# A modulation product on one Trainium2 core: from accumulated rows and TensorE sums to VectorE products with a running sum

## What is computed

```python
mod = jax.nn.silu(c) @ w_ada[i] + b_ada[i]
mod_c = jax.nn.silu(c_ctx) @ w_ada[i] + b_ada[i]
sh1, sc1, g1, sh2, sc2, g2 = jnp.split(mod[:, None, :], N_MOD, axis=-1)
csh1, csc1, cg1, csh2, csc2, cg2 = jnp.split(mod_c, N_MOD, axis=-1)
...
hc = modulate(rmsnorm(xc, norm1_g[i]), csh1, csc1)
k_c, v_c = jnp.split(hc @ w_in[i][:, NA_WIDTH:3 * NA_WIDTH], 2, axis=-1)
...
h = modulate(rmsnorm(x, norm1_g[i]), sh1, sc1)
...
x = x + g1 * gated_merge(gna, ghy, y_na, y_hy, w_na_o[i], w_hy_o[i], w_out[i])
h2 = modulate(rmsnorm(x, norm2_g[i]), sh2, sc2)
x = x + g2 * swiglu(h2, ffn_w1[i], ffn_w3[i], ffn_w2[i])
```

## Time and profile before

| | us |
|---|---|
| three runs | 1608.90, 1612.44, 1613.04; median 1612.44 |
| the profiled execution, its own time | 1610.57 |
| its span in the profile | 1608.8 |
| mean granted clock of TensorE | 0.99 |
| VectorE busy | 1002.3 |
| ScalarE busy | 692.4 |
| HBM read and written over the span | 179.67 MB and 21.00 MB, 125 GB/s |

### The profile page before, as it was taken

One profiled execution on the slowest core, in us unless ns is written; L12 is line 12 of the kernel. 1 busy time (PEld: TensorE's weight loads), 2 busy tenths in 40 slices (PEclk: granted clock), 3 DMA queues, 4 the chain that ended last, 5 costly groups with the idle time before them and its releaser, 6 DMA issues. The chain is left out here.

```text
span 1608.8 us, 21150 instructions
## 1 busy us (share of the span) xinstructions
PE 1558.5 (97%) x8536; PEld 1316.6 (82%) x8536; DVE 1002.3 (62%) x1453; ACT 692.4 (43%) x1020; POOL 428.8 (27%) x371
## 2 busy tenths in 40 slices
PE   6999998999999999999999999999999999999997
PEld 5768886788888887888988778887788999999886
DVE  7675457778887476334775643338855688885324
ACT  5644346736433333323533344443445544443322
POOL 0024325523421010100060022214442655550002
PEclk9999999999999899999999999999999999999999
DMA  7342112452444254231446433215462122224221
GB/s 301 105 144 92 70 69 79 158 214 74 157 163 151 105 209 156 106 105 57 152 157 247 123 103 108 105 40 184 136 220 90 54 104 105 106 106 157 82 76 53
DMA packets 46684, 202.05 MB, mean 126 GB/s; under 512 B 14480, under 2 KB 14736, under 8 KB 27962
## 3 DMA queue, kind: packets, MB, share of 16 engines
q1 hardware_dynamic: 37346, 172.04, 29.6%
q0 software_dynamic: 8704, 28.30, 4.9%
q10 hardware_dynamic: 536, 0.35, 0.1%
HBM read 179.67 MB, written 21.00 MB: 125 GB/s over the span
## 5 line engine op out<-in xcount | busy, mean ns | idle before, releaser
L572 PE MATMUL ps<-xh,whi 128*128 128x512 f32 (+1 forms) x1136 | 404.8, 356 | 11.3 <-DVE xl L1898 8.4
L574 PE MATMUL ps<-xh,wlo 128*128 128x512 f32 (+1 forms) x1136 | 397.7, 350 | 0.0
L573 PE MATMUL ps<-xl,whi 128*128 128x512 f32 (+1 forms) x1136 | 397.6, 350 | 0.0
L1854 DVE TENSOR_TENSOR wlo<-raw,whi 128x2048 fp32r<-128x2048 f32 x89 | 217.5, 2444 | 142.5 <-ACT whi L1218 142.4
L1218 ACT ACTIVATE whi<-raw 128x512 fp32r<-128x512 f32 (+1 forms) x191 | 233.0, 1223 | 156.8 <-PE ps L574 86.8
L572 PEld LDWEIGHTS ps<-xh,whi 128*128 128x128 f32 x1136 | 215.9, 190 | 51.3 <-issue 22.2
L574 PEld LDWEIGHTS ps<-xh,wlo 128*128 128x128 f32 x1136 | 216.4, 190 | 30.5
L573 PEld LDWEIGHTS ps<-xl,whi 128*128 128x128 f32 x1136 | 216.0, 190 | 28.2
L2733 POOL TENSOR_TENSOR act<-xr 128x512 f32<-128x512 f32 x22 | 40.0, 1818 | 199.7 <-DVE xr L2296 199.0
L2296 DVE SCALAR_TENSOR_TENSOR xr<-ps,pc,xr 128x511 f32<-128x511 f32 x88 | 65.2, 746 | 41.5 <-ACT xr L1218 39.9
L2629 DVE TENSOR_TENSOR wlo<-raw,whi 128x512 fp32r<-128x512 f32 x98 | 77.4, 820 | 0.7 <-ACT whi L1218 0.7
(11 more groups left out here) (477 smaller groups left out, 3497.0 us busy)
## 6 DMA issues: line engine op xcount, KB each, us to landing
raw<-in_w_in SPq DMA_DIRECT2D x35, 1024.0 KB, 5.2
raw<-in_ffn_w SPq DMA_DIRECT2D x33, 1024.0 KB, 4.8
raw<-in_ada SPq DMA_DIRECT2D x24, 1024.0 KB, 4.8
raw<-in_w_up SPq DMA_DIRECT2D x22, 1024.0 KB, 4.8
raw<-in_w_down SPq DMA_DIRECT2D x11, 1024.0 KB, 4.8
xd<-X POOLq DMA_DIRECT2D x8, 512.0 KB, 6.6
td<-vr POOLq DMA_DIRECT2D x16, 256.0 KB, 3.6
raw<-td SPq DMA_DIRECT2D x4, 1024.0 KB, 4.8
```

Source lines behind the costliest of these rows:

```text
L572: pe.e.matmul(o, lh, rh, start=start, stop=False)
L573: pe.e.matmul(o, lh, rl, start=False, stop=False)
L574: return pe.e.matmul(o, ll, rh, start=False, stop=stop)
L1854: up(ve.e.tensor_tensor(lo, raw[conv_at[j] % 3][:, :], hi.bitcast(F32), ALU.subtract), "wlo")
```

## The change

The modulation weight is stored transposed: a chunk now holds two blocks of 128 outputs (on the partitions) by 1,024 inputs. silu(c_ctx) and silu(c) are written once to a small HBM buffer `csd` (ScalarE, 2,048 single numbers), and read back as rows repeated on all partitions: `cb` (2,048 wide, in the buffer of `ch`) before the up stage, `cb2` (silu(c) alone, in the buffer of `xh`) after up tile 43. `ada(n)` is now two blocks with one `tensor_tensor_reduce` each (two in group 0: context and token), which multiplies chunk and row and leaves the sum over the inputs as a column of `mod` or `small`. The product itself goes back over the chunk (or into `spent`) and isn't used.

TensorE's sums are gone; `Fills.skip` moves the rotation on by as many banks as they took. The chunks of group 0 sit at up steps 4, 5, 7, 8, 10, 11, 13, 14, and the other 16 in the down stage (`ADA_DOWN`), behind the split of piece k + 4. The context's `channels(8)` and `(9)` move from after step 13 to after step 17. The gates are columns now, and ScalarE stores them to `gated` with two transfers of 1,024 single numbers, before the query copies. GpSimd's three kinds of gate transfers go, and its two row loads into `bc` come before the up stage.

```diff
@@ the plan
-ADA_UP = (1, 2, 3, 5, 6, 7, 9, 10, *range(12, 20))
-ADA_IN2 = (1, 2, 3, 4, 5, 5, 6, 6)
+ADA_UP = (4, 5, 7, 8, 10, 11, 13, 14)
+ADA_DOWN = (*range(4), *range(5, 10), *range(11, 18))
...
-    several("w_down", 11)
...
+    for i in range(11):
+        plan.append(("w", ins["w_down"][i]))
+        for n, k in enumerate(ADA_DOWN):
+            if k // 2 == i - 1:
+                plan.append(("ada", ins["ada"][8 + n]))
+    several("w_in2", 20)
@@ tensor_program: the sums, and where they were called
-            def ada(g):
-
-                b = take(("adc", g), "mod", (2, 5, 6)[g])
-                pe.wait_ge(sig["cst"], 1)
-                pe.wait_ge(sig["ada"], ada_no(8 * g + 7))
-                for o, src, n_ in ((0, acc_c, 16), (16, acc_x, 16)) if g == 0 else ((0, bc, 8),):
-                    c0 = 1024 if g == 1 else 0
-                    for i in range(n_):
-                        m = pe.e.matmul(b[:, o + i:o + i + 1], src[:, c0 + P * i:c0 + P * i + P], onesf[:, 0:1],
-                                        start=True, stop=True)
-                done(m, ("adc", g))
-                for h in range(2) if g else ():
-                    b = take(("adr", g, h), "adrow", 2 * (g - 1) + h + 1)
-                    c0 = 512 * h + (1024 if g == 2 else 0)
-                    done(pe.e.matmul(b[0:1, :], onesf[:, 0:1], bc[:, c0:c0 + 512], start=True, stop=True), ("adr", g, h))
...
-                        ada((11, 20).index(2 * j2 + part))
-                if j2 == 6:
+                        fills.skip(1 if j2 < 10 else 3)
+                if j2 == 8:
@@ scalar_program
+            ac.wait_ge(sig["cs"], 1)
+            ac.e.dma_start(bass.AP(csd.tensor, 0, [[1, P], [P, 16]]), cs[:, :], allow_slow_non_contiguous=True).then_inc(sig["brow"], 16)
...
+            ac.wait_ge(sig["brow"], 16)
+            ac.e.dma_start(cb, bass.AP(csd.tensor, 0, [[0, P], [1, 2 * D]])).then_inc(sig["brow"], 16)
...
-                    if inst == 0 and k == 3:
-                        ac.wait_ge(sig["gated"], 16)
...
+            tile(("up", 43))
+            ac.e.dma_start(cb2, bass.AP(csd.tensor, 0, [[0, P], [1, D]])).then_inc(sig["brow"], 16)
...
+            ac.wait_ge(sig["adrow"], 2)
+            for i in range(2):
+                ac.e.dma_start(bass.AP(gated.tensor, D * i, [[1, P], [P, 8]]),
+                               small[:, 257 + 8 * i:265 + 8 * i], allow_slow_non_contiguous=True).then_inc(sig["gated"], 16)
@@ vector_program, ada(n)
-                for dst, c in ((acc_c, 0), (acc_x, 8)) if g == 0 else ((bc, 0),):
-                    col = cs[:, c + k:c + k + 1]
-                    if k == 0:
-                        m = ve.e.tensor_scalar(dst[:, :], raw[i % 3][:, :], col, None, ALU.mult)
...
-                        m = ve.e.scalar_tensor_tensor(out=dst[:, :], in0=raw[i % 3][:, :], scalar=col, in1=dst[:, :],
-                                                      op0=ALU.mult, op1=ALU.add)
+                ve.wait_ge(sig["brow"], 32 if n < 8 else 48)
+                for b in range(2):
+                    w = r[:, D * b:D * b + D]
+                    if n < 8:
+                        ve.wait_ge(sig["ada"], ada_no(n - 1) - 3 + 2 * b if n else 0)
+                        for o, dst, c in ((0, spent[b], cb[:, 0:D]), (16, w, cb[:, D:2 * D])):
+                            col = o + 2 * n + b
+                            up(ve.e.tensor_tensor_reduce(dst, w, c, 1.0, 0.0, ALU.mult, ALU.add, mod[:, col:col + 1]), "ada")
                     else:
+                        up(ve.e.tensor_tensor_reduce(w, w, cb2, 1.0, 0.0, ALU.mult, ALU.add, ada_col(2 * n + b)), "ada")
@@ vector_program, pieces
                     if k + 4 < NFF:
                         one(k + 4)
+                    if inst == 0 and k in ADA_DOWN:
+                        ada(8 + ADA_DOWN.index(k))
@@ the weight as stored
-    g["ada"] = a["w_ada_2"][0].reshape(8, P, 3, 2048).transpose(2, 0, 1, 3).reshape(24, P, 2048)
+    g["ada"] = a["w_ada_2"][0].T.reshape(24, 2, P, D).transpose(0, 2, 1, 3).reshape(24, P, 2048)
```

More of the change, by code:

```diff
@@ L71, in group, with skip @@
         return 1
+    def skip(self, n, pool="all"):
+        self.turn[pool] += n
     def take(self, pe, key, sem, value, pool="all"):
@@ L125, in ada_no @@
 def ada_no(a):
-    return 2 * a + 2 if a < 8 else a + 9
-ADA_UP = (1, 2, 3, 5, 6, 7, 9, 10, *range(12, 20))
-ADA_IN2 = (1, 2, 3, 4, 5, 5, 6, 6)
+    return 4 * (a + 1) if a < 8 else 2 * (a + 1) + 16
+ADA_UP = (4, 5, 7, 8, 10, 11, 13, 14)
+ADA_DOWN = (*range(4), *range(5, 10), *range(11, 18))
 KC0 = (0, 8, 24, 32)
@@ L339, in build, with ada_col @@
         ncd = dram("ncd", [8, S])
+        def ada_col(i):
+            g, k = divmod(i, 8)
+            x, at_ = (mod, 8 * g + 8 + k) if g in (3, 4) else (small, 257 + k + (8 if g == 5 else 0))
+            return x[:, at_:at_ + 1]
         def pcol(name, i=0, rows=P):
@@ L1975, in ada @@
             def ada(n):
[L1977 removed]
                 i = ada_at[n]
+                r = raw[i % 3]
                 ve.wait_ge(raw_sem[i % 3], 16 * (i // 3 + 1))
[L1980 to L1986, removed]
[L1987 to L1995 removed]
+                ve.wait_ge(sig["brow"], 32 if n < 8 else 48)
[6 more added lines that the diff above has]
+                            up(ve.e.tensor_tensor_reduce(dst, w, c, 1.0, 0.0, ALU.mult, ALU.add, mod[:, col:col + 1]), "ada")
+                    else:
+                        up(ve.e.tensor_tensor_reduce(w, w, cb2, 1.0, 0.0, ALU.mult, ALU.add, ada_col(2 * n + b)), "ada")
             def ada_sums(g):
[L1998 removed]
                 ba, n1, n2 = PCOLS["b_ada"], PCOLS["norm1_g"], PCOLS["norm2_g"]
                 if g == 0:
+                    ve.wait_ge(sig["ada"], ada_no(7))
                     for o in (0, 16):
[L2002 removed]
+                        up(ve.e.tensor_tensor(mod[:, o:o + 16], mod[:, o:o + 16], pc[:, ba:ba + 16], ALU.add), "mod")
                     ve.wait_ge(sig["mod"], 2)
@@ L2007, in ada_sums @@
                     return
-                if g == 1:
-                    up(ve.e.tensor_tensor(mod[:, 32:40], b[:, 0:8], pc[:, ba + 24:ba + 32], ALU.add), "mod")
-                else:
-                    up(ve.e.tensor_tensor(mod[:, 40:48], b[:, 0:8], pc[:, ba + 32:ba + 40], ALU.add), "mod")
-                    ve.wait_ge(sig["mod"], 6)
-                    up(ve.e.scalar_tensor_tensor(out=mod[:, 40:48], in0=mod[:, 40:48], scalar=1.0, in1=pc[:, n2:n2 + 8],
-                                                 op0=ALU.add, op1=ALU.mult), "mod")
-                ve.wait_ge(sig["brow"], 16 * g)
-                r = row2 if g == 1 else row3
-                for h in range(2):
-                    b = tile(("adr", g, h))
-                    c = slice(512 * h, 512 * h + 512)
-                    up(ve.e.tensor_tensor(r[0:1, c], b[0:1, :], r[0:1, c], ALU.add), "adrow")
+                ve.wait_ge(sig["ada"], ada_no(23))
+                up(ve.e.tensor_tensor(mod[:, 32:40], mod[:, 32:40], pc[:, ba + 24:ba + 32], ALU.add), "mod")
+                up(ve.e.tensor_tensor(mod[:, 40:48], mod[:, 40:48], pc[:, ba + 32:ba + 40], ALU.add), "mod")
+                ve.wait_ge(sig["mod"], 6)
+                up(ve.e.scalar_tensor_tensor(out=mod[:, 40:48], in0=mod[:, 40:48], scalar=1.0, in1=pc[:, n2:n2 + 8],
+                                             op0=ALU.add, op1=ALU.mult), "mod")
+                for i, a in enumerate((16, 40)):
+                    x = small[:, 257 + 8 * i:265 + 8 * i]
+                    up(ve.e.tensor_tensor(x, x, pc[:, ba + a:ba + a + 8], ALU.add), "adrow")
             def gate_input(g, rows, bias):
@@ L2859, in gpsimd_program @@
                 affine(t)
+            po.wait_ge(sig["xb"], 4)
+            po.e.dma_start(bcg[:, :], rows_of(ins["rows"], 4)).then_inc(sig["rows"], 16)
+            po.e.dma_start(bcb[:, :], rows_of(ins["rows"], 5)).then_inc(sig["rows"], 16)
             for j2 in range(11):
```

57 lines of the change are left out of this document (10 added, 47 removed).

## The result

The changed kernel takes **1593.26 us** (median of 4 runs, 1591.28 to 1597.04), the kernel before 1611.78 us (4 runs, 1608.90 to 1613.04): a ratio of **0.9894, with a 95% interval from 0.988 to 0.9908**. The forecast was 1591.5 us, 0.9870 of the median it started from. Between the two medians lie 18.5 us, where a gain of 20.9 was predicted. The profiled execution took 1591.28 us, with a span of 1589.5: 19.3 us less than the span before.

A forecast was written before the change was run, and what follows sets the result against it. TensorE, busy 97% of the span, was taken as the bound. Gains of 13.5 + 3.7 + 3.7 = 20.9 us, with added work hidden, took 1612.4 to 1591.5 us; range 1586.5 to 1602.

The forecast's parts named there:

- Terms 1 to 3: At the three places where TensorE sums the modulation: removing the sums gains 13.5 + 3.7 + 3.7 = 20.9 us.
- Term 1: First group's sums at 516 us: 10.65 us of products plus 2.85 at the 1.2 GHz level, 13.5 us gained.
- The price of a product with running sum: On VectorE: 1,024 columns and the read of the sum take 0.69 + 0.53 + 0.08 = 1.30 us a piece.
- some 5 us more: VectorE's added work over all chunks, claimed hidden because VectorE isn't the bound.
- The rival of the slow product: VectorE's product is slow from SBUF: at 2.0 us a piece the whole gain is used up; chance 0.08.
- The cover in the up stage: Up stage: VectorE's chunk work stays hidden between low-half splits, with 1.4 us left at the tightest place; cost 0.
- The cover in the down stage: Down stage with 16 added chunks: VectorE does 8.9 us per 11.24 us period, splits and loads in time; cost 0.
- The rival of starving: Down stage: loads take 8 us instead of 4.8, 10 us lost, giving 1601.5 us; chance 0.10.
- The small transfers at 0: ScalarE's single-number transfers near 52 and 797 us: cost between 0 and 7 us, taken as 0.
- Whose waits are for work long done: Rotation of TensorE's eight banks: skipped places cost no instruction and keep the rotation, whose waits are already met.
- The move of the chunks: Group 0's chunks at other up steps, the other 16 in the down stage: nothing booked for moving them.
- The gain isn't kept: At the context's keys or attention TensorE arrives earlier but waits for the same end of another chain: 1612 us; chance 0.04.

The follow-up runs named there:

- experiment 1: Kernel before with TensorE's sums cut to one one-column product per accumulator and per row half, VectorE's multiply-adds kept: 1593.61 us, ratio 0.9897.
- experiment 2: Kernel before with only the first group's sums cut to one product per accumulator: 1601.02 us, ratio 0.9942.
- experiment 8: Changed kernel with group 0's chunks back at up steps 1, 2, 3, 5, 6, 7, 9, 10: 1600.10 us, ratio 0.9924.
- Experiment 6: Changed kernel with two more VectorE products per block in the up stage, doubling the work per chunk: 1625.70 us, ratio 1.0091.
- experiment 7: Changed kernel with one more VectorE product per block in the down stage: 1602.88 us, ratio 0.9946.
- experiment 5: Changed kernel without the skipped bank places, so every later bank is another one: 1599.84 us, ratio 0.9934.
- 9: Changed kernel with group 0's chunks at up steps 2, 3, 5, 6, 7, 9, 10, 11: 1590.74 us, ratio 0.9894.

## Why the prediction was right, step by step

- *Terms 1 to 3.* Right in sum: the pair at 947 us shows 20.6 us, once the lead of 0.24 from ahead of the places is taken off, where the sum less the wait is 20.5; experiment 1 gets the same time without anything else of the change. Term 1 alone: 13.5 of 13.5 in the changed kernel, 13.1 of 13.3 in experiment 2. That a clock at the 1.2 GHz level belonged to the sums' price is shown by experiment 2, in which it stays at 1.00. By the medians the gain is 18.5 us, 2.4 less than predicted; that the forecast is only 1.8 us from the measured time owes 0.7 us to luck, the median of three runs that it started from having been that much above the median of four.
- *The price of a product with running sum.* Right in kind, 13% too high: 1.30 us was 0.69 + 0.53 + 0.08, and from start to start it is 1.15. The product takes 1.22 us, the read lies beside the next one. A chunk of group 0 takes 4.58 us, not 5.2. The "some 5 us more" for VectorE isn't what the prediction's own prices add up to (8 x 0.5 + 16 x 0.2 is 7.2 us); the page shows 1.5. The rival of the slow product (from 2.0 us a piece) fell, but not by as much as the median says: beside GpSimd it takes 3.4 us (experiment 8), and one at 476.75 us of the changed kernel, beside GpSimd's multiplication into `act`, took 2.31.
- *The cover in the up stage.* Right: no wait from 404 to 620 us. Experiment 6 makes the same chain late by doubling the work, though not in four equal parts.
- *The cover in the down stage.* Right in direction, with a wait of 0.4 us; its slack was worked out too small (experiment 7: 9.6 us for an expected 15). The rival of starving fell: the loads of `w_down` land in 5.2 us (median), not 8.
- *The small transfers at 0.* Right: their issues take 0.41 us and 1.01 us for two, inside idle time that didn't grow. The Trainium skill ("DMA: Bandwidth & Descriptors", Rules for kernel authors) speaks against a strided last dimension; the extra packets are there, 4,432 of them where the single numbers are 4,096, but on no path. Queue q10 of the page (packets, MB, share of the DMA engines) had 536 packets before and has now:

```profile
q10 hardware_dynamic: 4968, 1.94, 0.5%
```

- *"Whose waits are for work long done".* This was said of the bank rotation, and holds only because the change keeps it. It was an explanation too weak for what the skipped places do: without them one wait is 7.24 us (experiment 5).
- *The move of the chunks.* The prediction booked nothing for it. Right for the change as made, but the old places would have cost 6.8 us with the new product (experiment 8). I had looked at VectorE's load there, not at what GpSimd does beside it.
- *"The gain isn't kept".* It fell as a whole; 1.5 of the 20.8 us were given back behind 1080 us, in a place that the prediction didn't name. Nearly all of it goes at two waits: 0.8 us at that for `yy`, behind a store that lands later in every trace with the new modulation, and 0.6 us at that for `wlo L1854`, which varies by execution and also comes without the change. The prediction booked nothing for either. The clock has no part in it in this pair of traces.

## What to carry to other kernels

If TensorE is the bound, price small sums on it by the gap that they leave between full products and by the clock behind them, not by their arithmetic: here 32 of them cost 13 us, while 64 products of 1,024 columns on an engine at 63% made TensorE wait 0.4. Before such work moves to VectorE, look at what GpSimd does in the same stretch: the place of one chunk decided over a third of the gain. And when instructions that take a bank are removed, keep the rotation of the others until a run shows that it doesn't matter: without it this kernel lost 6.6 us.

## What the runs showed of the hardware

- A VectorE product with two inputs in SBUF took 3.41 us instead of 1.22 while GpSimd ran an addition of 1,024 columns (2.8 us each), and GpSimd's eight additions took 25.31 us instead of 22.64. The Trainium skill ("SBUF — State Buffer", Who interferes with whom) says that a VectorE instruction with two SBUF inputs contends with a GpSimd instruction that reads SBUF; the traces of experiments 8 (3.41 us, beside the additions) and 9 (1.22 us, behind them) agree. The size, 2.8 times, I had not expected.
- One-column products on TensorE: 16 sums (32 products) took 3.63 us, and the granted clock was 0.51 to 0.58 for some 3 us behind them; 8 sums at a time left it at 1.00; 32 sums (64 products) in a row brought it to 0.50 at 525 to 530 us.
- Falls of the granted clock to 0.5 to 0.9 over stretches of 5 us, behind short waits of TensorE at a few fixed places of the program (near 371, 1098, 1130 and 1257 us of the changed kernel), in some executions and not in others. The spread of the runs (1589.8 to 1597.0 us over eight of the changed kernel) is of the size that they explain.
- One store of GpSimd (`gd<-tm`), in flight together with a load of 1 MiB, took 6.5 to 8.9 us to land, where the median of the 16 was 2.8 to 3.0.
